# Input projections of a hybrid decoder step as three products of split operands, with the weights split in place

## The reference

```python
h = rms_norm(x, lw['attn_norm'])
proj = h @ lw['w_in']                      # 1024 x (1024 + 3*768 + 4) columns
p_rwkv = proj[..., :N_RWKV_COLS]           # 1024 columns, feed the RWKV-7 group
q, k, v = ...                              # 12 heads of 64 each; q and k of 8 heads are RMS-normed
f_logit = proj[..., N_RWKV_COLS + 3 * a_w:]
xm = p + (prev - p) * mu                   # in the RWKV group: prev is the token before
...
x = x + mix @ lw['w_out']
x = x + jnp.square(jax.nn.relu(h2 @ lw['w_mlp_up'])) @ lw['w_mlp_down']
```

## Time and profile before

| | us |
|---|---|
| median of 3 runs | 1074.85 |
| profiled execution, its own time | 1072.73 |
| its span, first to last instruction | 1071.1 |
| TensorE busy | 1008.2 (94%) |
| VectorE busy | 402.9 (38%) |
| ScalarE busy | 347.2 (32%) |
| mean granted TensorE clock | 0.97 of full |

### The profile page before, as it was taken

How to read it: one execution, slowest core, us unless ns; L and a number is a source line. 1 busy time by engine, 2 the same in 40 slices (tenths; PEclk the granted TensorE clock), 3 DMA queues, 4 the chain that set the end, 5 groups by cost and what they waited for, 6 DMA issues and landing times.

```text
span 1071.1 us, 20339 instructions
## 1 busy us (share of the span) xinstructions
PE 1008.2 (94%) x8560; PEld 776.6 (73%) x8560; DVE 402.9 (38%) x762; ACT 347.2 (32%) x612; POOL 56.3 (5%) x108
## 2 busy tenths in 40 slices
PE   6999999898998979889879999999999999999998
PEld 4776655557897756666644448999777799997776
DVE  3006142924565664564381234332113132221212
ACT  3002422311432266675360113644211134441110
POOL 0000000113400000013410000000000000000000
PEclk9999999999898899799969999999999999999999
DMA  9202301003000358457989102222122252211222
GB/s 327 95 14 69 104 15 51 34 34 102 7 4 3 111 189 289 154 179 267 342 335 319 65 1 79 80 80 79 40 79 79 79 158 80 79 40 42 89 92 103
DMA packets 58044, 117.46 MB, mean 110 GB/s; under 512 B 4906, under 2 KB 30026, under 8 KB 57826
## 3 DMA queue, kind: packets, MB, share of 16 engines
q1 hardware_dynamic: 51714, 93.05, 25.8%
q0 software_dynamic: 6240, 23.12, 6.2%
HBM read 109.62 MB, written 6.53 MB: 108 GB/s over the span
## 4 chain that ended last, share of the span: by engine, by line
PE 87%; DVE 5%; ACT 3%; issue 2%; DMA 2%; SPq 1%; DVEq 0%; ACTq 0%
PE PS L748 12%; PE PS L1157 11%; PE PS L1158 11%; PE PS L1159 11%; PE PS L830 7%; PE PS L734 6%; PE PS L1127 5%; PE PS L995 3%; PE PS L1230 3%; PE PS L1063 2%; PE PS L1017 2%; PE PS L958 2%; PE PS L752 2%; PE PS L973 1%; PE PS L982 1%
## 5 line engine op out<-in xcount | busy, mean ns | idle before, releaser
L2061 DVE TENSOR_TENSOR WL<-Wraw,WH 128x2048 fp32r<-128x2048 f32 x32 | 73.4, 2292 | 164.5 <-ACT WH L1463 164.5
L1157 PE MATMUL PS<-h2H,WH 128*128 128x288 f32 x448 | 132.8, 296 | 0.0
L1158 PE MATMUL PS<-h2L,WH 128*128 128x288 f32 x448 | 132.2, 295 | 0.0
L1159 PE MATMUL PS<-h2H,WL 128*128 128x288 f32 x448 | 131.7, 294 | 0.0
L748 PE MATMUL PS<-W,HM 128*128 128x384 f32 (+1 forms) x384 | 126.5, 490 | 0.0
L1463 ACT ACTIVATE WH<-Wraw 128x2048 fp32r<-128x2048 f32 x32 | 61.0, 1907 | 165.8 <-DMA Wraw<-in_w_mlp_down 141.1
L748 PEld LDWEIGHTS PS<-W,HM 128*128 128x128 f32 x384 | 73.0, 191 | 50.6 <-issue 1.2
L1157 PE MATMUL PS<-WH,uH 128*128 128x512 f32 x256 | 101.4, 396 | 1.8 <-issue 1.8
L1158 PE MATMUL PS<-WL,uH 128*128 128x512 f32 x256 | 99.8, 390 | 0.0
L1159 PE MATMUL PS<-WH,uL 128*128 128x512 f32 x256 | 99.6, 389 | 0.0
L1157 PEld LDWEIGHTS PS<-h2H,WH 128*128 128x128 f32 x448 | 83.9, 187 | 0.6 <-issue 0.6
(11 more groups left out here) (311 smaller groups left out, 1363.8 us busy)
## 6 DMA issues: line engine op xcount, KB each, us to landing
AR<-in_cache_kv SPq DMA_DIRECT2D x76, 384.0 KB, 4.2
AR<-in_cache_kv POOLq DMA_DIRECT2D x44, 384.0 KB, 4.7
Wraw<-in_w_mlp_up SPq DMA_DIRECT2D x16, 1024.0 KB, 5.4
Wraw<-in_w_mlp_down SPq DMA_DIRECT2D x16, 1024.0 KB, 4.9
W<-in_w_in SPq DMA_DIRECT2D x5, 1536.0 KB, 6.4
VQ<-in_x_prompt SPq DMA_DIRECT2D x8, 512.0 KB, 8.5
W<-in_w_out SPq DMA_DIRECT2D x2, 2048.0 KB, 12.0
W<-in_w_in SPq DMA_DIRECT2D x2, 1024.0 KB, 12.2
```

Source lines behind the costliest of these rows:

```text
L1157: mm(out, lH, rH, start=start, stop=False)
L1158: mm(out, lH, rL, start=False, stop=False)
L1159: return mm(out, lL, rH, start=False, stop=stop)
L2061: tt(WL[:, q % 2, :], Wraw[:, q % 2, :], WH[:, q % 2, :].bitcast(F32), SUB).then_inc(w_lo, 1)
```

## The change

Both input projections use `mm3` with operands of type float32r. The normed rows are split per tile into `HR` (high, ScalarE, `split_rows`) and `hL` (low, VectorE, `rows_low`). The weights come in nine pieces (384, 384, 256, then six of 384 or 388 columns); there are two places. A piece's high part (`piece_high`, ScalarE) goes beside the raw one, and its low part (`piece_low`, VectorE) over the raw one. The sample rows of q, k and v keep plain float32 products on raw weights, so `tile(g, 4)` runs before the low part of that piece is written. The first piece is loaded and split in three parts of 128 columns. A piece is loaded when the last tile of the piece two before it is done. Token differences and mix are computed per group of 128 columns (`mix(m)`). The transposes of q and k go through four PSUM banks, and in another place of the order. `V` stays in `ring`, `X4` takes its old place, 1280 columns of the constants `rc` are loaded only after the last tile (the low rows lie there before), and a few entries of `PLAN` are moved by one or two places.

```diff
+        P_COLS = [(0, QC), (QC, QC), (2 * QC, N_RW - 2 * QC)]
+        P_COLS += [(N_RW + g * QC, QW[g]) for g in range(6)]
+        P_LAST = {0: 3, 1: 6, 2: 8}
+        QKV = [(0, 4)]
+        for g in range(6):
+            mine = [(g, t) for t in range(4)]
+            if g < 5:
+                mine.insert(2 if g == 0 else 3, (g + 1, 4))
+            QKV += mine
+        def piece_used(i):
+            return (p_ps, P_LAST[i]) if i < 3 else (qkv_ps, N_AT[i - 3, 3] + 1)
# SP
-            def load_w(n):
-                if n >= NW:
-                    sp.wait_ge(*used(n - NW))
...
+            def load_piece(i):
+                if i >= 2:
+                    sp.wait_ge(*piece_used(i - 2))
+                c0, cols = P_COLS[i]
+                sp.dma_start(piece_raw(i), w_in[:, :, c0:c0 + cols]).then_inc(in_w[i % 2], 16)
...
+            for n in range(3):
+                cols = slice(n * 128, (n + 1) * 128)
+                sp.dma_start(piece_raw(0)[:, :, cols], w_in[:, :, cols]).then_inc(in_wp[n], 16)
+            load_piece(1)
+            sp.dma_start(rc[:, 0:RC_KEPT], d["rc"][:, 0:RC_KEPT]).then_inc(in_rc, 16)
...
             sp.wait_ge(qkv_ps, 30)
+            sp.dma_start(rc[:, RC_KEPT:], d["rc"][:, RC_KEPT:]).then_inc(in_rc, 16)
             sp.dma_start(Wf[:, prompt_c:prompt_c + N_PC], d["pcst"]).then_inc(in_pc, 16)
-            sp.wait_ge(tr_ps, 20)
-            sp.wait_ge(k_out, 16 * 10)
             sp.dma_start(X4[:, 0:1024], d["s0"]).then_inc(in_s0, 16)
...
             sp.wait_ge(stored, 16 * 12)
+            sp.wait_ge(yt_ps, NB_G)
             for i, (t0, nr) in enumerate(TILES):
                 sp.dma_start(x2[0:nr, i, :], xrows(i)).then_inc(in_resid, 16)
# PE
+            def tile(g, t):
+                n, i = N_AT[g, t], g + 3
+                if n >= 4:
+                    pe.wait_ge(qkv_ev, n - 3)
...
+                if t == 4:
+                    piece_wait(pe, i)
+                elif t == 0:
+                    pe.wait_ge(g_hi, 3 + i)
+                    pe.wait_ge(g_lo, 3 + i)
+                for k in range(KT):
+                    if t < 4:
+                        last = mm3(PS[:, bank:bank + QW[g]], normed(k, slice(t0, t0 + nr)),
+                                   (piece_hi(i)[:, k, :], piece_lo(i)[:, k, :]), k == 0, k == KT - 1)
+                        continue
...
+            def mixed_half(m, a):
+                i, c = m // 3, slice((m % 3) * 128, (m % 3 + 1) * 128)
+                if m < 3 or m % 3 == 0:
+                    pe.wait_ge(g_hi, m + 1 if m < 3 else 3 + i)
+                    pe.wait_ge(g_lo, m + 1 if m < 3 else 3 + i)
...
+            pe.wait_ge(hT_ready, 3)
+            mixed_half(0, 0)
+            turn_row(4)
+            mixed_half(1, 0)
+            pe.wait_ge(hT_ready, 5)
+            mixed_half(0, 1).then_inc(p_ps, 1)
+            mixed_half(1, 1).then_inc(p_ps, 1)
+            for m in range(2, 8):
+                if m == 7:
+                    tile(0, 4)
+                mixed_half(m, 0)
+                mixed_half(m, 1).then_inc(p_ps, 1)
...
+            for g in (3, 4):
+                for t in range(3):
+                    tile(g, t)
+                turn_qk(g - 1, range(4))
+                tile(g + 1, 4)
+                turn_qk(g - 1, [4])
+                tile(g, 3)
+            for t in range(4):
+                tile(5, t)
# ACT, order at the start
+            for i in range(3):
+                row_deviation(i)
+            split_rows(0)
+            row_deviation(3)
+            split_rows(1)
+            row_deviation(4)
+            first_high(0)
+            split_rows(2)
+            first_high(1)
+            split_rows(3)
+            split_rows(4)
+            first_high(2)
+            piece_high(1)
# DVE
+            def rows_low(i):
+                dve.wait_ge(h_hi, i + 1)
+                for n, k in enumerate((slice(0, 6), slice(6, 8))):
+                    ins = tt(hL[n][:, :, t0:t0 + nr], hf[:, i % 2, k, 0:nr], HR[:, k, t0:t0 + nr].bitcast(F32), SUB)
+                ins.then_inc(hT_ready, 1)
+            def piece_low(i):
+                dve.wait_ge(g_hi, 3 + i)
+                if i >= 3:
+                    dve.wait_ge(qkv_ps, N_AT[i - 3, 4] + 1)
+                tt(piece_lo(i), piece_raw(i), piece_hi(i).bitcast(F32), SUB).then_inc(g_lo, 1)
+            for i in range(4):
+                scale_input(i)
+                if i:
+                    take_turned(i - 1)
+                if i >= 2:
+                    rows_low(i - 2)
+            first_low(0)
+            rows_low(2)
+            scale_input(4)
+            first_low(1)
+            take_turned(3)
+            take_turned(4)
+            rows_low(3)
+            rows_low(4)
+            first_low(2)
+            piece_low(1)
...
+            for m in range(5):
+                mix(m)
+            piece_low(2)
+            mix(5)
+            mix(6)
+            piece_low(3)
+            mix(7)
...
             norm_scale(2)
+            sums(3, 0)
+            sums(3, 1)
+            sums(3, 2)
+            take_qk(2, range(5))
+            piece_low(7)
+            sums(3, 3)
+            norm_scale(3)
...
                         if kind == "L":
+                            dve.wait_ge(in_rc, 32)
```

More of the change, by code:

```diff
@@ new lines, in mixed_half @@
+            def mixed_half(m, a):
[3 more added lines that the diff above has]
+                    pe.wait_ge(g_lo, m + 1 if m < 3 else 3 + i)
+                if m >= 3:
+                    pe.wait_ge(p_ready, m - 2)
+                out = pair((m + 1) % 3 + 1)
+                for k in range(KT):
+                    last = mm3(out[:, a, :], (piece_hi(i)[:, k, c], piece_lo(i)[:, k, c]),
+                               normed(k, slice(a * 288, (a + 1) * 288)), k == 0, k == KT - 1)
+                return last
@@ L798, in _ @@
                 last.then_inc(lora_ps, 1)
-            gemm(4)
-            pe.wait_ge(lora_ev, 6)
-            turn_qk(0)
-            gemm(2)
+            tile(0, 0)
+            pe.wait_ge(p_ready, 8)
+            for m in range(8):
+                last = turn(PS[0:9, 2048 + m * 128:2048 + (m + 1) * 128], pT[:, m, SEQ - 1:T:DT], ident)
+            last.then_inc(shift_ps, 1)
+            tile(0, 1)
+            tile(1, 4)
+            for j, x in ((0, (0, 2)), (2, (0, 3)), (4, (1, 0))):
+                lora_product(j)
+                lora_product(j + 1)
+                tile(*x)
+            tile(1, 1)
+            pe.wait_ge(lora_ev, 6)
+            turn_qk(0, range(4))
+            tile(1, 2)
+            turn_qk(0, [4])
+            tile(2, 4)
+            tile(1, 3)
+            tile(2, 0)
             pe.wait_ge(kksq_ready, 1)
@@ L1320, in _ @@
                 f(slot(dst), slot(src), ACT.Exp, scale=sign).then_inc(exp_out, 1)
-            take(3)
-            deviations(3)
-            take(5)
+            take(3, 0)
+            take(3, 1)
+            piece_high(7)
+            take(3, 2)
+            take(4, 4)
+            take(3, 3)
+            deviations(3)
+            take(4, 0)
+            take(4, 1)
+            piece_high(8)
+            take(4, 2)
+            take(5, 4)
+            take(4, 3)
+            for t in range(4):
+                take(5, t)
             act.wait_ge(logf_in, 1)
@@ L1620, in take_qk @@
                     ins.then_inc(tr_ev, 1)
-            norm_sums(0)
+            for x in ((0, 4), (0, 0), (0, 1)):
+                sums(*x)
+            piece_low(4)
+            for x in ((1, 4), (0, 2), (0, 3)):
+                sums(*x)
             norm_scale(0)
-            norm_sums(1)
+            sums(1, 0)
+            take_qk(0, range(4))
             dve.wait_ge(lora_ev, 6)
@@ L1633, in _ @@
             tt(slot(12), slot(11), slot(11), MUL).then_inc(kksq_ready, 1)
+            sums(1, 1)
+            piece_low(5)
+            take_qk(0, [4])
+            sums(1, 2)
+            sums(2, 4)
+            sums(1, 3)
             dve.wait_ge(shift_out, 32)
@@ L1674, in _ @@
             link(tt(slot(4), slot(4), slot(2), MUL))
+            take_qk(3, range(5))
+            piece_low(8)
             link(tt(slot(9), slot(9), slot(11), MUL))
```

447 lines of the change are left out of this document (245 added, 202 removed).

## The result

The changed kernel took 1039.1 us (median of 4 runs) against 1073.6 in the same session, ratio 0.9672 [0.9632, 0.9712]. The forecast was 1038.9. In all 15 runs of it that were made, in three sessions, the median is 1035.5 (1030.2 to 1042.5), against medians of 1072.1 to 1073.6 for the kernel before in the same sessions: about 37 us less, where 36.0 were forecast. The profiled execution has a span of 1039.8 us.

A forecast was written before the change was run, and what follows sets the result against it. The prediction took TensorE's own list to bound the kernel up to the recurrence; -11.1 - 26.4 + 4.7 + 1.5 + 1.8 - 8.0 + 0.75 + 0.8 = -36.0 us, from 1074.85 to 1038.9 us. The range was 1029 to 1052.

The forecast's parts named there:

- mixed products: 128 mixed-column products of 288 columns: from 0.487 us each to three float32r products of 0.1333 us, -11.1 us.
- tiles: 192 products for rows of q, k, v: 126.5 us now, 100.1 as three float32r products each, -26.4 us.
- start and clock: Before TensorE's first product: splits on ScalarE and VectorE delay it, +4.7 us; slower clock after the idle stretch, +1.5 us.
- waits for pieces: TensorE waiting for loaded and split weight pieces: +0.4 at piece 3, +0.9 and +0.5 at piece 7, sum +1.8 us.
- waits that go: TensorE's waits in the projection stage, nearly all around the transposes of q and k, disappear: -8.0 us.
- handover to ScalarE: End of the stage: TensorE waits for ScalarE to copy the last tile, plus forget column and handover, +0.75 us.
- late constants: Late part of `rc`, asked for at the last tile's end, arrives after VectorE wants it: +0.8 us (0 to 3).
- behind the stage: From the recurrence's beginning to the end: the same 820 us as now; a change over 3 us would show it wrong.
- The main term: Both input projections, three float32r products for each plain float32 one: mixed products -11.1 us, tiles -26.4 us.
- The walk along the lists: Weight pieces followed: late at 3 (+0.4 us) and 7 (+0.9); 4, 5, 6, 8 ready 0.2 to 4 early.
- Rivals 2 to 5: 2: start loses only 2 us, chance 0.11; 3: shorter 384-column step, 0.03; 4: places starve, 0.03; 5: clock or step bad, 0.02.
- Three of the signs: Profile after: first product at 21 to 22 us, recurrence at 213 to 217, then the same 820 us to the end.

The follow-up runs named there:

- e6_plain: Changed kernel with one plain float32 product of the high parts in place of the three of split operands, splits and order kept; 1068.6 us.
- e4_low_late: Changed kernel with one more VectorE pass over each weight piece just ahead of its low part; 1056.1 us.
- e5_before_banks: Kernel before with only the four PSUM banks for the transposes of q and k; 1068.7 us, ratio 0.9952.
- e1_again: Changed kernel unchanged, run for a second profile; 1036.6 us, ratio 0.9667 against the kernel before.
- f1_changed: Changed kernel unchanged, as base for others on the same chip and a third profile; 1035.3 us.
- e7_best: Changed kernel with the PLAN of before, ten identity transposes ahead of the first mixed product and the first column group computed pass by pass; 1031.3 us.
- f4_start_old_plan: Changed kernel with ten added transposes, first column group pass by pass and the PLAN of before, second time; 1031.1 us.
- e2_old_plan: Changed kernel with the PLAN of before; 1030.3 us.
- f3_start_new_plan: Changed kernel with ten added transposes and first column group pass by pass, keeping the new PLAN; 1031.1 us.
- f2_old_plan: Changed kernel with the PLAN of before, second time; 1034.9 us.
- e3_warm: Changed kernel with 27 identity transposes into an unused PSUM bank ahead of the first mixed product; 1032.7 us.

## Why the prediction was right

| step of the forecast | forecast | measured | by |
|---|---|---|---|
| mixed products | -11.1 | -11.1 | steps of 0.133 |
| tiles | -26.4 | -25.8 | 160 x 0.523 + 32 x 0.531 = 100.7, from 126.5 |
| start and clock | +6.2 | +5.4 (6.4 to 6.9 where tile 3 was slow) | two half groups done at 29.25, 23.82 without delay |
| waits for pieces | +1.8 | +0.2 | one wait, piece 3 |
| waits that go | -8.0 | -8.0 | none left of the earlier trace rows |
| handover to ScalarE | +0.75 | +0.7 | first L925 |
| late constants | +0.8 | 0 | gaps of 0.60 and 0.49 there, 1.50 and 0.6 before |
| behind the stage | 0 | -0.7, +1.0, +8.3 | three profiles |

This is the first profile. The 0.531 is three times the 0.177 at which the 388-column products step. The 23.82 is 17.42 plus 6.4 us for two half groups. The terms ahead of "late constants" sum to -38.6; the profile has -39.55, and the 1 us between was not traced further. The forecast's own sum holds; its chances for a faster kernel add up to 0.96 and not 0.95.

- The main term was right in both ways, by the step in the trace and by e6_plain, which took it back and lost 34.1 us of the stage. That is 2.8 under the 36.9 of the steps. Of these, 1.1 are the clock's: the group of tiles at 196 to 218 took 21.84 us and the others at 384 columns 20.64 to 20.84, and the forecast divided all of them by the number of products. At full clock a plain product of 384 columns steps by 0.645 to 0.651. Where the rest of the 2.8 lies was not traced.
- The start was mis-sized by 0.8 us: I let the third low row part end at 21.4, and it ended at 20.2. The x tiles landed 0.4 us earlier, and short steps of ScalarE and VectorE overlap in the trace; how much each made was not taken apart. The clock's price was forecast at 1.5; fifteen products at 0.24 instead of 0.133 make 1.6. That price is right for the two profiles where TensorE had come to full speed by tile 3. In the other executions it was slow from the first transposes on, and 20 to 24 slow products cost 2.1 to 2.6 us, which the forecast did not think of.
- The walk along the lists named the right places, but for piece 4, which had 10.2 us of room. Piece 3's wait is there (0.2, forecast 0.4). At piece 7 ScalarE took tile (3,0) at 160.9 and the high part at 162.4; I had 162 for the first, and the low part was done at 171.73 instead of 173.9, 0.35 us before its use at 172.08, where the forecast had it 0.9 too late. It is the tightest piece, as forecast, without a wait. e4_low_late shows the margins to be thin.
- The waits around the transposes: e5_before_banks shows that the banks alone bring 5.9 us of the stage, 3.0 of them in waits. The other 5.0 us of waits are gone in the changed kernel as well, by the new order as far as can be said, for no run changed the order alone. The forecast had them as one term, and had no term for the clock that comes back with them.
- Rivals 2 to 5: the start cost 5.4 us and not 2; 384 columns step as the line says (0.1743) and not by 0.1625; the pieces didn't starve; the clock was full in the products behind the start.
- The late part of `rc` landed 4.1 us after its issue at 210.7, and VectorE began with it at 214.92, when its PSUM input was there too. The term was 0.
- Behind the stage the forecast said 0 with 3 us either way. The scatter is larger: 815.7 to 828.4 us over the profiles of the table. I had taken one execution of before as the base; that its behind was 820.1 and in the middle was luck.
- Three of the signs that the forecast gave missed in the first profile: the first product began at 20.2 us (21 to 22 said), the recurrence at 211.4 (213 to 217 said), and the part behind changed by 8.3 us, over the 3 us that it named as a sign of being wrong. The last one was that execution's, as e1_again and f1_changed show; the first two are the start and the pieces, sized too dear.

The hit on the median to 0.2 us in the first session is partly chance: a stage 3.6 us better, and behind it an execution 8.3 us worse. Against the median of all runs, 1035.5, the forecast is 3.4 us too high, about the stage's surplus of the first profile; but it was also added to a median of before, 1074.85, that lies 2 us above the kernel's later ones.

What stays open: why cache pages come late in some executions and not in others. The stretches at 391 to 431 and 491 to 551 us have the DMA engines nearly full in the kernel before as well (shares of 0.89 and 0.95), and no run here changed their load. Open too is why TensorE has full speed at tile 3's transposes in some executions of one kernel and not in others (e7_best and f4_start_old_plan are the same kernel).

## What to carry to other kernels

A plain float32 product steps here by 0.650 us at 384 columns, as long as four products of one column a cycle at 2.4 GHz (0.640) and a little. Three float32r products of split operands cost 0.80 of it at 384 columns and 0.82 at 288. That pays only while TensorE sets the end, and the splits (2.8 us on ScalarE, 3.4 on VectorE for 128x3072) must be laid where the weights' raw form is not wanted any more and early enough: here with 0.35 to 0.76 us to spare at four pieces. Give TensorE something to do in an idle stretch of 3 to 4 us ahead of dense work, or begin with the passes whose operands are ready first. Read its speed from the steps, since the column of the granted clock said 1.00 over products at half speed. And before an order change is called a gain, run it on two bases and twice: most of the 6 us of e2_old_plan did not come again.

## What the runs showed of the hardware

- Behind 3.6 us without work, TensorE ran at 1.2 GHz for 3.8 us (15 products from 20.23 to 24.0, e1_again the same), though it had been at full speed before. With ten transposes of a constant in that stretch it stayed at 2.4 GHz (e7_best, f3_start_new_plan). In the kernel before, two banks more for the transposes did the same at 194 us.
- In other executions of the changed kernel and its variants TensorE was still at half speed at 15.5 to 17.5 us (eight transposes in 1.97 us and not 1.09) and stayed there through the first 20 to 24 products, while the granted clock is given as 1.00 (f1_changed, e2_old_plan, f2_old_plan, e4_low_late). 27 transposes of a constant brought it to full speed in time (e3_warm); after ten the first pass of eight products took 1.58 us and not 1.32, and the next one was at full speed (f4_start_old_plan).
- A float32r product has a step of 0.417 ns a column and 13 to 14 ns beside it at 288, 384 and 512 columns, in two different places of the program. The Trainium skill ("TensorE: Matmul & The Clock Gate", Back-to-back issue gap) gives N / 2.4 + 2.5 ns for the isolated gap between warm matmuls; the steps of the float32r products here, each with a weight load of its own, are 11 to 12 ns longer.
- At the same DMA share of 1.0 and some 370 GB/s (475 to 479 us in the first profile and e1_again), TensorE waited up to 4.2 us for a cache page in one execution of the changed kernel and 2.1 in the next two.
